# The second modulation chunk of five pairs is multiplied and summed on GpSimd instead of VectorE

## What is computed

```python
c_act = jax.nn.silu(c)
for l in range(DEPTH):
    mod = c_act @ ada_w[l] + ada_b[l]          # 1024 numbers by a matrix of 1024 x 6144
    sh1, sc1, g1 = ...                         # six pieces of mod, 1024 each
    h = rmsnorm(x, norm1_g[l]) * (1.0 + sc1) + sh1
    x = x + g1 * token_mix(h, ...)             # starts with the projections h @ w_in[l]
    h = rmsnorm(x, norm2_g[l]) * (1.0 + sc2) + sh2
    x = x + g2 * grouped_moe(h, ...)
```

## Time and profile before

| | |
|---|---|
| median of three runs | 1925.69 us |
| the profiled execution's own time | 1925.36 us |
| its span, first to last instruction | 1923.6 us |
| PE busy | 1810.6 us (94% of the span) |
| DVE busy | 925.6 us (48%) |
| POOL busy | 25.1 us (1%) |
| chain that ended last | PE 83%, DVE 10%, ACT 2%, DMA 2% |
| the five pairs and their projections | from 44 to 129 us |

### The profile page before, as it was taken

How to read it: one execution, slowest core, us unless ns; L and a number is a source line. 1 busy time by engine, 2 the same in 40 slices (tenths; PEclk the granted TensorE clock), 3 DMA queues, 4 the chain that set the end, 5 groups by cost and what they waited for, 6 DMA issues and landing times.

```text
span 1923.6 us, 46301 instructions
## 1 busy us (share of the span) xinstructions
PE 1810.6 (94%) x21084; PEld 1573.1 (82%) x21084; DVE 925.6 (48%) x1650; ACT 371.9 (19%) x723; POOL 25.1 (1%) x24
## 2 busy tenths in 40 slices
PE   5999987999998999997999998998999989999999
PEld 3678676899997688686899996667888988878899
DVE  4878877200005867865000004675677661133355
ACT  3013242100002022322000014263211110021110
POOL 0000200000000000200000000000000000000000
PEclk8999998999999999998999999999999999999999
DMA  9995447699995682643999994102888653434330
GB/s 359 387 386 198 176 174 308 236 391 423 421 413 215 232 322 75 219 181 145 373 400 424 420 400 148 63 27 75 293 300 284 209 176 132 148 128 162 129 113 24
DMA packets 180604, 465.90 MB, mean 242 GB/s; under 512 B 5152, under 2 KB 55936, under 8 KB 172288
## 3 DMA queue, kind: packets, MB, share of 16 engines
q1 hardware_dynamic: 180192, 463.83, 64.6%
q10 hardware_dynamic: 288, 0.26, 0.0%
HBM read 463.03 MB, written 1.05 MB: 241 GB/s over the span
## 4 chain that ended last, share of the span: by engine, by line
PE 83%; DVE 10%; ACT 2%; DMA 2%; issue 1%; SPq 0%; ACTq 0%; DVEq 0%
PE pair L398 81%; DVE AR L1575 2%; DMA ring<-in_ada_w 2%; DVE XH L1575 1%; PE pair L1045 1%; DVE RST L1637 1%; DVE AR L1821 1%; ACT AR L1290 0%; DVE AR L1831 0%; SPq L289 0%; PE pair L902 0%; DVE AR L1835 0%; ACT AR L1329 0%; DVE XH L1822 0%; PE pair L659 0%
## 5 line engine op out<-in xcount | busy, mean ns | idle before, releaser
L398 PE MATMUL pair<-XH,ring 128*128 128x256 f32 (+1 forms) x3328 | 747.9, 386 | 21.1 <-ACT XH L1191 17.2
L398 PEld LDWEIGHTS pair<-XH,ring 128*128 128x128 f32 (+1 forms) x3328 | 626.8, 190 | 131.6 <-issue 38.6
L398 PE MATMUL pair<-AR,ring 128*64 128x88 f32 (+2 forms) x14336 | 696.6, 249 | 16.7 <-issue 9.3
L398 PEld LDWEIGHTS pair<-AR,ring 128*64 128x64 f32 (+1 forms) x14336 | 667.5, 139 | 40.1 <-issue 20.1
L2074 DVE TENSOR_TENSOR AR<-AR,pair 128x352 f32<-128x352 f32 x32 | 16.7, 521 | 398.4 <-PE pair L398 398.4
L1575 DVE SCALAR_TENSOR_TENSOR AR<-ring,CACT,AR 128x512 f32<-128x512 f32 x245 | 184.2, 752 | 8.7
L398 PE MATMUL pair<-AR 128*64 128x128 f32 (+3 forms) x1600 | 132.0, 292 | 8.0 <-ACT AR L1462 3.3
L398 PEld LDWEIGHTS pair<-AR 128*64 128x64 f32 (+3 forms) x1600 | 106.2, 146 | 17.8 <-issue 4.5
L2277 DVE SCALAR_TENSOR_TENSOR AR<-pair,VEC,AR 128x255 f32<-128x255 f32 x88 | 41.9, 476 | 95.8 <-ACT AR L1487 95.8
L1394 ACT ACTIVATE AR<-pair 128x352 f32 (+1 forms) x64 | 26.3, 465 | 300.7 <-PE pair L398 300.7
L1487 ACT ACTIVATE AR<-pair,VEC 128x256 f32<-128x256 f32 x88 | 36.6, 466 | 213.9 <-PE pair L398 213.9
(11 more groups left out here) (268 smaller groups left out, 1125.6 us busy)
## 6 DMA issues: line engine op xcount, KB each, us to landing
ring<-in_ada_w SPq DMA_DIRECT2D x48, 2048.0 KB, 13.7
ring<-in_w_gate SPq DMA_DIRECT2D x32, 2048.0 KB, 10.9
ring<-in_w_up SPq DMA_DIRECT2D x32, 2048.0 KB, 11.0
ring<-in_w_down SPq DMA_DIRECT2D x32, 2048.0 KB, 11.6
ring<-in_ffn_w_up SPq DMA_DIRECT2D x44, 1024.0 KB, 7.6
ring<-in_w_in SPq DMA_DIRECT2D x18, 2048.0 KB, 15.2
ring<-in_ffn_w_down SPq DMA_DIRECT2D x8, 2048.0 KB, 8.6
ring<-in_sc_w_in SPq DMA_DIRECT2D x6, 2048.0 KB, 8.0
```

Source lines behind the costliest of these rows:

```text
L398: return pe.matmul(o, lhsT, rhs, start=start, stop=stop, **kw)
```

## The change

Of each pair ahead of `hq`, `hi`, `hg`, `lat1` and `lat2` the second chunk is now GpSimd's. It multiplies the eight pieces in place in the ring (eight `tensor_scalar` of 128 x 512), then adds halves: 128 x 2048, 128 x 1024, and 128 x 512 into the same place of `AR` as before, each addition behind a wait on its own semaphore `pool_step`. It reports on `rows_pool`, and PE waits for that at the second turn. Before a chunk it waits for the slot's arrival and for PE's turn of the second chunk of the pair before. DVE leaves the five chunks out. To have two semaphores free, three small loads share one (`tables_in`), and two loads of the second block share another (`second_in`).

```diff
+POOL_ADA = [BEFORE[name, 0][1] for name in ("hq", "hi", "hg", "lat1", "lat2")]
+DVE_ADA = [m for m in ADA_NO if m not in POOL_ADA]
...
-                    no = ADA_NO[a, l, k]
-                    pe.wait_ge(s["rows_summed"], no + 1)
+                    if (a, l, k) in POOL_ADA:
+                        pe.wait_ge(s["rows_pool"], POOL_ADA.index((a, l, k)) + 1)
+                    else:
+                        pe.wait_ge(s["rows_summed"], DVE_ADA.index((a, l, k)) + 1)
...
-                pe.wait_ge(s["router_in"], 16)
+                pe.wait_ge(s["tables_in"], 48)
...
-            pe.wait_ge(s["const2_in"], 16)
+            pe.wait_ge(s["second_in"], 32)
...
                 for job in jobs:
-                    sum_rows(*job)
+                    if job not in POOL_ADA:
+                        sum_rows(*job)
...
         @block.gpsimd
         def _(pool):
+            pool.wait_ge(s["cact_ready"], 1)
+            before, n = FIRST_ADA[3], 0
+            for a, l, k in POOL_ADA:
+
+                c = CHUNK_OF["ada", (a, l, k)]
+                pool.wait_ge(full[c % RING], 16 * (c // RING + 1 + extra(c)))
+                pool.wait_ge(s["multiplied"], CHUNK_OF["ada", before] + 1)
+                w, acc = ring[c % RING][:, :].rearrange("p (t n) -> p t n", t=KT), acc_of(a, l, k, 0)
+                for t in range(KT):
+                    ins = pool.tensor_scalar(w[:, t, :], w[:, t, :], CACT[:, a, t, 0:1], None, ALU.mult)
+                for h in (4, 2, 1):
+                    n += 1
+                    ins.then_inc(s["pool_step"], 1)
+                    pool.wait_ge(s["pool_step"], n)
+                    o = w[:, 0:h, :] if h > 1 else acc.rearrange("p (a n) -> p a n", a=1)
+                    ins = pool.tensor_tensor(o, w[:, 0:h, :], w[:, h:2 * h, :], ALU.add)
+                ins.then_inc(s["rows_pool"], 1)
+                before = (a, l, k)
```

More of the change, by code:

```diff
@@ L253, in stack_program @@
         FOLDED = (1, 3, 6, 7, 8)
-        names = """multiplied const1_in levels_in const2_in vec_in router_in x_in ctx_in pos_in out_stored
+        names = """multiplied const1_in tables_in second_in vec_in x_in pos_in out_stored
         dve_step
-        cact_ready rows_summed mod_taken coef_ready rope_ready lb_ready angle_ready
+        cact_ready rows_summed rows_pool pool_step mod_taken coef_ready rope_ready lb_ready angle_ready
         cz_ready row_ready squares_ready folded sums_ready std_ready scaled_ready h_act h_dve x_done out_tile ctx_squares
@@ L266, in stack_program @@
         zeroed gather_ready lower_ready rt_part rt_copied rt_ready rt_sig diag_ready cbc_ready cbc_copied sg_ready gu_ready he_ready
-        slots_in iota_in sel_ready places_ready overflow_ready off_ready h_turned ht_ready
+        iota_in sel_ready places_ready overflow_ready off_ready h_turned ht_ready
         perm_ready placed_ready xs_ready xs_act xs_dve xs_padded st_turned st_copied
@@ L302, in _ @@
             sp.dma_start(POS.bitcast(I32), T["pos"]).then_inc(s["pos_in"], 16)
-            sp.dma_start(LVM, T["levels"]).then_inc(s["levels_in"], 16)
-            sp.dma_start(CS[:, C_U:C_U + P], T["before"]).then_inc(s["slots_in"], 16)
+            sp.dma_start(LVM, T["levels"]).then_inc(s["tables_in"], 16)
+            sp.dma_start(CS[:, C_U:C_U + P], T["before"]).then_inc(s["tables_in"], 16)
             sp.wait_ge(s["zeroed"], 2)
-            sp.dma_start(WR[:, :, 0:NE], T["w_router"].rearrange("(t p) n -> p t n", p=P)).then_inc(s["router_in"], 16)
+            sp.dma_start(WR[:, :, 0:NE], T["w_router"].rearrange("(t p) n -> p t n", p=P)).then_inc(s["tables_in"], 16)
             proj = dict(hf=512, hq=0, hi=1024, hg=1536, lat1=2048, lat2=2560, gt0=2720, gt1=3232, gt2=3744, gt3=4256)
@@ L347, in _ @@
                     sp.wait_ge(s["st_copied"], DEPTH)
-                    sp.dma_start(CS[:, C1_OVER:C1_OVER + N_C2], T["const2"]).then_inc(s["const2_in"], 16)
-                    sp.dma_start(X2[:, :, S:2 * S], T["ctx"].rearrange("(t p) n -> p t n", p=P)).then_inc(s["ctx_in"], 16)
+                    sp.dma_start(CS[:, C1_OVER:C1_OVER + N_C2], T["const2"]).then_inc(s["second_in"], 16)
+                    sp.dma_start(X2[:, :, S:2 * S], T["ctx"].rearrange("(t p) n -> p t n", p=P)).then_inc(s["second_in"], 16)
             for k in range(3):
@@ L782, in broadcast @@
                             .then_inc(s["cbc_ready"], 1)
-                pe.wait_ge(s["slots_in"], 16)
+                pe.wait_ge(s["tables_in"], 48)
                 pe.wait_ge(s["sel_ready"], l + 1)
@@ L1413, in _ @@
             multiplied(ck("moe", 1) + 45)
-            act.wait_ge(s["ctx_in"], 16)
+            act.wait_ge(s["second_in"], 32)
             A(CTXQ, X2[:, :, S:2 * S], ACT.Square).then_inc(s["ctx_squares"], 1)
@@ L1825, in masked @@
                     if n == 0:
-                        V.wait_ge(s["levels_in"], 16)
+                        V.wait_ge(s["tables_in"], 48)
                     o = PB if n % 2 == 0 else PD
@@ L2100, in _ @@
             scaled(5, X2[:, :, S:2 * S], H2[:, :, S:2 * S], RST[:, S:2 * S], 1, 0, 0, 1)
-            V.wait_ge(s["const2_in"], 16)
+            V.wait_ge(s["second_in"], 32)
             wcos, wsin = [CS[:, C1_OVER + d:C1_OVER + d + S].rearrange("p (a n) -> p a n", a=1) for d in (D_COS, D_SIN)]
```

## The result

The changed kernel takes **1969.09 us**, median of four runs (1966.36 to 1972.53), against 1925.2 (1924.66 to 1927.82, four runs): ratio 1.0214 [1.0200, 1.0227]. It is slower, as forecast, but by 43.9 us where the forecast had about 18, and above the range, which ended at 1964. Rival B, at 1972.5, came nearest. The profiled execution took 1971.04 us, with a span of 1969.2, 45.6 more than before.

What follows compares the result with a forecast made beforehand. PE, busy 94% of the span, bounds the kernel, so only what makes it late costs time. 1925.36 + 16.7 (lat2's later turn) + 1.1 (clock) = 1943.2, with the median's offset 1943.5 us; range 1930 to 1964.

Steps and rivals of the forecast that it cites:

- Rival B: GpSimd's multiplications cost 1.83 us each, by own work or alternation with DVE; chunk 23.1 us, kernel 1972.5 us; chance 0.15.
- the mechanism: Five pairs: GpSimd's round of 17.85 us exceeds the 16.4 between landings; lat2's turn comes 16.7 us later, all reaching the end.
- restarts: Between GpSimd's chunks: it may restart once PE has turned the last one, 0.55 us each, four times.
- the free semaphores: Small loads at the kernel's start and in the second block: sharing their semaphores costs nothing.
- the additions: GpSimd's halving sums, 3584 elements per partition and chunk: twice the copy's rate, 8.5 us.
- the loads that may slip: Projection weights of the five pairs: loads may slip by 10 us and still arrive before POOL is done.
- I take 1.1 ... Eight: 8.8 us: GpSimd's 128x512 multiplications: 1.1 us each, between copy's 0.61 and tensor_scalar's 1.83; eight per chunk 8.8 us (4.9 to 14.6).
- P: GpSimd's time for one chunk, multiplications plus additions: 17.3 us (9.2 to 27.4), against DVE's 5.95.
- the clock: PE after the pause before lat2's second turn: lower granted clock costs 1.1 us more.
- DVE's relief: Five chunks of 5.95 us leave DVE, 30 us in all; worth at most 7.4 us to the kernel.
- Rival A: GpSimd multiplies at the copy's rate, not held up by DVE; chunk 13.4 us, kernel 1933.7 us; chance 0.20.
- Rival C: Not slower: GpSimd's multiplications and additions run at 1.19 ns an element; chunk 9.2 us, kernel 1928.7 us; chance 0.06.

Runs made afterwards that it cites:

- 2: Changed kernel with only lat2's second chunk on GpSimd instead of five chunks: 1943.05 us, ratio 1.0077 to the kernel before.
- 7: Changed kernel with GpSimd's last addition left in the ring's slot and turned from there, without the wait for the place in AR: 1967.43 us, one run.
- 10: Changed kernel with GpSimd taking the first chunk of each of the five pairs and VectorE the second: 1967.22 us, ratio 1.0213 to the kernel before.
- 3: Changed kernel with only hq's second chunk on GpSimd instead of five chunks: 1937.56 us, ratio 1.0039 to the kernel before.
- 1: Changed kernel with no chunk on GpSimd, only the shared semaphores kept: 1927.77 us, ratio 0.9998 to the kernel before.
- Experiment 5: Changed kernel with two 128x2048 multiplications by one constant per chunk instead of eight of 128x512, factors left out: 1974.82 us, one run.
- 6: Changed kernel with one two-input 128x4096 multiplication per chunk, factors broadcast, instead of eight tensor_scalar: 1963.87 us, ratio 1.0183 to the kernel before.
- 4: Changed kernel with VectorE doing only one of eight pieces of each pair's first chunk, the rest left out: 1965.38 us, one run.
- 8: Changed kernel with each second chunk split, six pieces on VectorE and two on GpSimd, PE adding both sums: 1937.15 us, ratio 1.0055 to the kernel before.
- 9: Changed kernel with nothing on GpSimd, shared semaphores kept, the five second turns made twice (20 more small matmuls): 1936.58 us, ratio 1.0056 to the kernel before.

## Why the prediction was right and wrong

**Right: the mechanism.** GpSimd is slower than the loads, falls behind, and the turn of lat2 carries the sum of its rounds to the end. With measured sizes the same sum gives the measured turn: start 49.79, chunks 20.67 + 22.44 + 22.22 + 21.88 + 21.88 = 109.09, restarts 0.92 + 3 x 0.91 = 3.65, together 162.53; PE turned at 162.58. Experiments 2, 7 and 10 moved a term each, and the turn moved with it; 3 showed that an early pair's lateness is in part won back (13.9 us at hq's projection, 10.5 at lat2's), so that it is the lateness of the last pair that counts in full. Also right: the free semaphores (1), the additions (8.15 us where 8.5 was taken; 4551, 2337 and 1260 ns), the loads that may slip, and POOL's old work far behind. The size of the additions was in part luck: they were put at twice the copy because they read two inputs, but the multiplication, with one, costs more for each element (1.54 against 1.26 us for 512). For the additions the 7.9 us estimated from the Trainium skill (GPSIMD Engine Reference, section 3.1) was as near; the trace's 4551 ns agrees with that page's 4497 to 1.2%.

**Wrong: the step "I take 1.1 ... Eight: 8.8 us".** A multiplication measured 1.54 us undisturbed and 1.70 in the mean, 12.3 to 13.9 us per chunk. The prediction placed it just above the copy's rate and counted the tensor_scalar of 2x512 (1.83) as an upper end because of its short pieces. It was the other way round: of the rows at hand, the one of the same operation was near, 3.57 ns an element against 3.0 measured, and the one of the longer but other operation was far, 1.19. Experiment 5 shows the price to belong to the elements, so shape was no reason to leave that row.

The miss at lat2's turn, 162.5 against 137.7, is 24.8 us. Forty multiplications took 67.1 us instead of 44.0: 23.1 of it, 17.7 by their own price (61.7 at 1.54) and 5.4 beside DVE. The restarts add 1.4 (0.91 against 0.55), the start 0.8 (49.8 against 49.0, the wait for the slot included), and the additions give 0.5 back.

**Too small: the clock.** The prediction took 1.1 us after the last pause. From lat2's turn to gt0's projection it was 8.03 us before and 10.10 after, 2.1 us of loss: the pauses are now 5 to 6 us instead of 2.6, and the granted clock around one of them, over 90 to 100 us, is 0.66.

**Too much: DVE's relief.** 30 us were to leave DVE; 19 did. Its remaining sums take 774 ns instead of 752, and L1765, L1770 and the first piece of a chunk are stretched beside POOL. It is off the path and costs nothing here, but in 5 and 6 it became the path.

**Rival A fell** with the copy's rate: 3.0 ns an element is far from one. The rule of the Trainium skill (GPSIMD Engine Reference, section 4.1) that one-input operations are "roughly line-rate" doesn't hold for this one: 1.54 us for 512 elements is also slower than the two-input product at 1.72 ns an element. The same section's advice to leave elementwise work to VectorE holds: 20.7 us against 5.95 for a chunk.

**Rival B was the case that came**, 1972.5 against 1969.1 (lat2's turn at 166.7 against 162.6), with 1.70 for its 1.83. Its first reason ("by its own work") carries it; its second, the alternation with DVE, is worth 5 of the 44 us (4). Giving B 0.15 and ending the range at 1964 was the error of judgement: P was bounded only by 9.2 and 27.4, each microsecond of P counts five times at the end, and the forecast's own band of 15.5 to 19.5 was narrower than the rows allowed.

**Rival C** would have needed a chunk under 10 us; none of the runs came near (15.5 at the best, in 6).

No version here beats the kernel before. Its whole prize was 7.4 us, and even a GpSimd chunk that keeps pace (6) takes longer than the 5.95 us that it replaces and holds up VectorE on the way. Fusing multiplication and addition on GpSimd wasn't tried.

## What to carry to other kernels

Price an operation on GpSimd from the row of the same operation, even in another shape, before one of another operation: here copy, tensor_scalar and the two-input product take 1.2, 3.0 and 1.7 ns an element, and the row of the same operation was off by 0.3 us (1.83 for 1.54) where the copy's was off by 0.9 (0.61). Where a helper's service time is longer than the interval of arrivals, every error in that time is multiplied by the number of rounds, so widen the range by as much. And before work is moved to GpSimd, ask which short VectorE instruction on the path can come to stand behind a long GpSimd one.

## What the runs showed of the hardware

- GpSimd's `tensor_scalar` with one input costs more than its two-input `tensor_tensor`: 3.0 ns an element at 512 and 2.66 at 2048, against 1.72 at 4096 for the product with spread factors, and 2.2 to 2.5 for additions of 2048 to 512 elements (4.55 and 1.26 us).
- A long GpSimd instruction can hold up even the shortest VectorE operation: a 128x4 addition took 6.80 us beside a 7.02 us product (6). The Trainium skill (SBUF — State Buffer, section Who interferes with whom) has a rule for that, two SBUF inputs against a GpSimd read, blocked for the whole instruction, and here the trace agrees. The same section counts `tensor_scalar`, though it has one input, among the operations that can take the shared ports and then contend, and the trace agrees there too: L1765 and L1577 were stretched (13.71 us for four, 5.57 for one, in 5). Not everything is held up: the transpose out of PSUM at 100.44, beside GpSimd's 128x2048 addition from 100.39 on, took its usual 0.32 us (6).
- Two pieces of a chunk on GpSimd stretch VectorE's six to what eight take alone (6.04 against 5.95 us, 8).
- Twenty more small matmuls before 125 us cost 10 us between medians and 8.1 between the profiled executions; 6.0 of these were found some 800 us later, in PE's unexplained pauses between 880 and 1040 us (9).
- TensorE's granted clock fell to 0.50 in a stretch of 10 us in which only GpSimd worked, and each full projection behind a wait of 5 us or more took 15.6 to 16.8 us where before hg's and lat1's, without a wait ahead of them, took 14.08.
